# Six places for the first modulation units, the projection weights in four transfers, and the bias lines inside its first tile

## The chip, the cores and the metric

The kernel runs on one core of a Trainium2 chip. The metric is device time in microseconds (us) of one execution. An execution of this kernel is a chain over five engines: TensorE (PE, with its weight loads as PEld), VectorE (DVE), ScalarE (ACT), GpSimd (POOL) and SyncE (SP), which here only issues transfers. Transfers issued by SP and ACT are listed as hardware queues q1 and q10, those issued by POOL as q0; all of them run on the same 16 DMA engines.

## The reference

One decoder layer for 512 prompt tokens and 8 sample tokens, width 1024, all in float32. In short:

```
mod = silu(c) @ w_ada + b_ada            # 9 rows of c, w_ada 1024 x 6144; six parts: sh, sc, g and sh_f, sc_f, g_f
h   = rms_norm(x) * (1 + sc) + sh        # 520 tokens
q, k, v, u = split(h @ w_in)             # w_in 1024 x 1280
attn = sliding window attention with sinks and a relative bias; pool = causal means of u
x   = x + g * (concat(attn, pool) @ w_out)
y   = x + g_f * moe(rms_norm(x) * (1 + sc_f) + sh_f)     # top 4 of 32 experts, w1 1024 x 2048, w2 1024 x 1024
```

The change touches what leads up to `h @ w_in` and that product's first tile of tokens.

## The kernel before, in words

The program has two parts with a barrier of all engines between them: `head`, all up to the routing, and `experts`. Nothing in `experts` is changed. Each engine has its own list of instructions, written out by hand, and runs it in order; semaphores (`wait_ge`, `then_inc`) tie the lists together.

**Modulation.** `w_ada` is loaded in 24 units of 1 MB, each 512 rows by 512 columns; two units make a chunk of 512 modulation columns. Chunks 0 to 3 (units 0 to 7, `WHOLE`) are shift and scale of the mixer and are needed before any projection. `load_ada` (L551) puts unit n into place n modulo 3 (`ADA_SLOTS`) of the ring `m.raw`, and waits from unit 3 on until the products of unit n - 3 are done (`ada_used`). TensorE multiplies a unit in `ada(n)` (L1342, matmul L1351), four products that stand beside each other in a bank; `mod_row(c)` (L1019) adds the bias row and the four partial rows on VectorE (L1028, L1032); `turn_mod(c)` (L1368, transposes L1372) turns the row on TensorE. When chunk 3 is turned, VectorE copies everything to `modT` (L1070) and forms `g1T`. The bias rows come in `m.bada`, 1024 columns at a time, each reload waiting until the rows before have been used.

**Tokens.** The tokens are loaded as four tiles of 128 and one of 8 (`load_x`), normed on ScalarE (L820 to L827, reciprocal on VectorE L1045), turned on TensorE (`turn_x`, L1364) and copied to `hT` by ScalarE (L833) and VectorE (L1048). TensorE's list takes `ada(t)` and `turn_x(t)` in turns, then `ada(5)`.

**Bias lines.** For each of the 8 heads one product of 33 rows by 383 columns (L1389) gives the head's relative bias as a line; VectorE copies it to `m.line` (L1064), with two banks in turn; a ninth product (L1391) gives `bias64`. TensorE's list has these nine between `turn_mod(1)` and `turn_mod(2)`, ahead of `ada(6)` and `ada(7)`. POOL later writes the lines to memory (`skew`, L688) and reads them back shifted (L695) for the scores.

**Projection.** `w_in` comes as one transfer of 5 MB (L580), issued behind unit 7. TensorE waits for it, then runs tile t = 0 to 3: eight steps k, each a product of 512 columns (L1437) and one of 256 (L1438) for q, k and v. VectorE has made `hT` for step k just before (L1082: scale and shift, eight instructions). Then come the samples, and u for all tokens (L1449).

**POOL.** Twelve small tables are loaded at the start (L666). When `w_in` has landed POOL loads the expert biases `m.bb`, clears `yd` in memory, copies caches, and writes `skew`.

## Time and profile before

| | us |
|---|---|
| median of 3 runs | 1385.18 (1381.89, 1385.18, 1388.03) |
| the profiled execution | 1384.42 |
| its span in the profile | 1382.7 |
| PE busy | 1221.5 (88%) |
| DVE busy | 669.8 (48%) |
| ACT busy | 490.1 (35%) |
| POOL busy | 215.4 (16%) |
| DMA, mean | 348 GB/s, 481.25 MB |

The span is what the profile sees of the execution; 1.7 us lie around it. Busy times are sums over the whole span, and stages with quite different limits are mixed in them, so the argument reads stages and waits rather than these sums. "idle before" in a line of the timeline is the time that the engine stood still ahead of it, with what released it; `<-issue` means that nothing in the profile shows what it waited for.

### The profile page before, as it was taken

Reading aid. Unit: us, or ns where it says so; the run is one execution under the profiler, and the core shown is the slowest. Engines: PE = TensorE matmul, PEld = TensorE weight load, DVE = VectorE, ACT = ScalarE, POOL = GpSimd, SP = SyncE. Lnnn points to the kernel's source line nnn. Section 1 sums busy time; section 2 is a strip of 40 time slices with the busy share of each in tenths; the row PEclk is TensorE's granted clock in tenths of the full one; section 3 lists DMA queues with packets and bytes.
Section 4 is the critical chain, followed back from the end, with each engine's and each line's share of the span. In section 5 each row is a group of like instructions: output and inputs, shape, how many; then the busy total and the mean of one; then the engine's idle time right before and its main releaser. Section 6 shows DMA issues by size and latency. Waiting matters only on the chain.

```text
span 1382.7 us, 17472 instructions
## 1 busy us (share of the span) xinstructions
PE 1221.5 (88%) x6463; PEld 725.0 (52%) x6463; DVE 669.8 (48%) x970; ACT 490.1 (35%) x703; POOL 215.4 (16%) x285
## 2 busy tenths in 40 slices
PE   4899779979999979999899889999789999999770
PEld 2364445543565735756674247555457654747320
DVE  2532664453675864543784134435334444837303
ACT  5011342230554633332663033333323343736300
POOL 3211321032111112102211101021111021111001
PEclk9699899989999999999999999999889999999885
DMA  9940686459999999999999999999999999999994
GB/s 297 380 135 5 237 286 228 159 220 400 360 401 366 404 403 389 402 389 344 410 412 401 400 389 406 387 347 405 405 389 400 386 363 411 406 411 403 412 391 181
DMA packets 113658, 481.25 MB, mean 348 GB/s; under 512 B 12497, under 2 KB 13824, under 8 KB 83820
## 3 DMA queue, kind: packets, MB, share of 16 engines
q1 hardware_dynamic: 100460, 451.52, 82.4%
q0 software_dynamic: 12768, 27.47, 7.5%
q10 hardware_dynamic: 344, 1.12, 0.3%
q8 instruction: 53, 0.87, 0.3%
q14 instruction: 33, 0.27, 0.1%
HBM read 463.46 MB, written 24.14 MB: 353 GB/s over the span
## 4 chain that ended last, share of the span: by engine, by line
PE 53%; DMA 13%; SPq 5%; DVE 5%; issue 1%; ACT 1%; POOLq 0%; ACTq 0%; DVEq 0%
PE bank L2302 50%; DMA raw<-in_w 9%; SPq L526 3%; DVE rawr L2141 2%; PE bank L2349 1%; DMA yd<-ost,slot_tok 1%; SPq L536 1%; DMA yd<-gu,slot_tok 1%; PE bank L2326 1%; ACT hi L1970 1%; DVE gu L2105 1%; SPq L532 1%; DMA xg_even<-h2d,slot_tok 0%; DVE gu L2103 0%; DVE yf L2295 0%
## 5 line engine op out<-in xcount | busy, mean ns | idle before, releaser
L2141 DVE TENSOR_TENSOR rawr<-raw,hi 128x1024 fp32r<-128x1024 f32 x288 | 341.5, 1222 | 125.0 <-ACT hi L1970 121.8
L1970 ACT CAST hi<-raw 128x1024 fp32r<-128x1024 f32 x288 | 295.4, 1049 | 153.9 <-PE bank L2302 113.8
L2302 PE MATMUL bank<-raw,xT_even 128*64 128x512 f32 (+1 forms) x704 | 138.0, 613 | 4.8 <-DMA raw<-in_w 4.7
L2302 PE MATMUL bank<-raw,aT 128*32 128x256 f32 (+1 forms) x992 | 109.6, 456 | 14.8 <-DMA raw<-in_w 14.6
L1862 POOL DMA_INDIRECT yd<-ost,slot_tok x31 | 54.4, 1756 | 362.6 <-ACT ost L1953 362.6
L2302 PE MATMUL bank<-raw,xT_odd 128*32 128x512 f32 (+1 forms) x544 | 88.0, 668 | 18.0 <-DMA raw<-in_w 18.0
L2302 PE MATMUL bank<-hi,aTh 128*128 128x512 f32 x240 | 78.7, 410 | 18.8 <-DVE rawr L2141 18.8
L2302 PE MATMUL bank<-hi,xTh_even 128*128 128x512 f32 x256 | 83.3, 407 | 5.3 <-DVE rawr L2141 5.3
L2103 DVE TENSOR_SCALAR gu<-bank 128x512 f32<-128x512 f32 (+1 forms) x50 | 31.4, 628 | 104.8 <-PE bank L2302 104.8
L1938 ACT ACTIVATE gu<-gu 128x512 f32<-128x512 f32 (+1 forms) x50 | 29.2, 583 | 144.1 <-DVE gu L2103 144.1
L2302 PE MATMUL bank<-rawr,xTh_even 128*128 128x512 f32 x256 | 80.1, 394 | 0.0
L2302 PE MATMUL bank<-hi,xTl_even 128*128 128x512 f32 x256 | 79.9, 393 | 0.0
L2302 PEld LDWEIGHTS bank<-raw,aT 128*32 128x32 f32 (+1 forms) x992 | 40.9, 120 | 74.1 <-issue 36.3
L2302 PE MATMUL bank<-hi,xTh_odd 128*128 128x512 f32 x224 | 73.5, 410 | 5.5 <-DVE rawr L2141 5.5
L2302 PE MATMUL bank<-rawr,aTh 128*128 128x512 f32 x240 | 76.3, 400 | 0.0
L2302 PE MATMUL bank<-hi,aTl 128*128 128x512 f32 x240 | 76.1, 399 | 0.0
L2302 PEld LDWEIGHTS bank<-raw,xT_even 128*64 128x64 f32 (+1 forms) x704 | 35.2, 127 | 68.2 <-issue 57.4
L2302 PE MATMUL bank<-rawr,xTh_odd 128*128 128x512 f32 x224 | 70.6, 397 | 0.0
L2302 PE MATMUL bank<-hi,xTl_odd 128*128 128x512 f32 x224 | 69.9, 394 | 0.0
L1953 ACT ACTIVATE ost<-bank,slot_gate 128x512 f32<-128x512 f32 (+1 forms) x43 | 26.0, 633 | 122.6 <-PE bank L2302 111.9
L2159 DVE SCALAR_TENSOR_TENSOR aTl<-bank,aTh 128x512 fp32r<-128x512 f32 x30 | 20.7, 689 | 97.8 <-ACT aTh L1931 97.8
L2302 PEld LDWEIGHTS bank<-hi,aTh 128*128 128x128 f32 x240 | 45.2, 194 | 34.4 <-DVE rawr L2141 23.2
(363 smaller groups left out, 1681.3 us busy)
## 6 DMA issues: line engine op xcount, KB each, us to landing
raw<-in_w SPq DMA_DIRECT2D x356, 1024.0 KB, 18.3
raw<-in_w_ada SPq DMA_DIRECT2D x24, 1024.0 KB, 7.1
raw<-in_w SPq DMA_DIRECT2D x48, 512.0 KB, 11.8
w_in_sb<-in_w_in SPq DMA_DIRECT2D x1, 5120.0 KB, 17.3
w_out_sb<-in_w_out SPq DMA_DIRECT2D x4, 1024.0 KB, 7.1
early<-in_w SPq DMA_DIRECT2D x4, 1024.0 KB, 12.4
xs<-in_x_prompt SPq DMA_DIRECT2D x4, 512.0 KB, 15.8
yd<-zero POOLq DMA_DIRECT2D x4, 512.0 KB, 10.5
```

The source lines that it names most:

```text
L526: sp.dma_start(raw.rearrange("p (k n) -> p k n", k=2), src).then_inc(landed, 16)
L532: sp.dma_start(raw[:, kk * D:(kk + 1) * D].rearrange("p (h c) -> p h c", h=2), src[:, :, j * 512:(j + 1) * 512]).then_inc(landed, 16)
L536: sp.dma_start(raw, src).then_inc(landed, 16)
L1862: gp.indirect_dma_start(yd_of[n], bass.IndirectOffsetOnAxis(ap=m.slot_tok[:, p % 6, b:b + 1], axis=0), out_rows(p, b), None, bounds_check= ...
L1938: nc.scalar.activation(gate, gate, ACT.Silu, scale=ALPHA).then_inc(silu_ready, 1)
L1953: done = nc.scalar.activation(out_rows(p, b)[:, n * w:(n + 1) * w], src, ACT.Copy, scale=m.slot_gate[:, p % 6, b:b + 1])
L1970: nc.scalar.copy(m.hi[:, (2 * n + h) % HI, :], m.raw[:, slot, h * D:(h + 1) * D]).then_inc(hi_done, 1)
L2103: v.tensor_scalar(gate, g, LIMIT, None, ALU.min).then_inc(gmin_ready, 1)
L2105: v.tensor_scalar(up, u, LIMIT, -LIMIT, ALU.min, ALU.max).then_inc(gu_free, 1)
L2141: v.tensor_tensor(m.rawr[slot][:, half], m.raw[:, slot, half], m.hi[:, (2 * n + h) % HI, :].bitcast(F32), ALU.subtract).then_inc(lo_done, 1)
L2159: v.scalar_tensor_tensor(m.aTl[:, k:k + n, :].rearrange("p k n -> p (k n)"), bank[7][:, 0:n * P], 1.0 / ALPHA, m.aTh[:, k:k + n, :].bitcas ...
L2302: return nc.tensor.matmul(out, lhsT, rhs, start=start, stop=stop, skip_group_check=True)
```

## The change

- `w_ada` units 0 to 5 get six places: the three of before and three more in memory that is free at that time (`m.ada_more`). Unit 6 and 7 go to places 0 and 1; units from 8 on rotate over three places as before, and wait for the same products as before.
- SP's list: units 0 to 4 and token tiles 0 to 4 in turns, units 5 to 7, then `w_in` as four transfers of two steps each with a semaphore each, then unit 8. The waits on `c_tr` and on the bias rows between units are gone from this stretch.
- The bias rows for chunks 0 to 3 (2048 columns) are one early transfer on ACT's queue into `m.bada_01`; `m.bada` serves the later chunks.
- TensorE's list: `ada(6)`, `turn_mod(2)`, `ada(7)`, `turn_mod(3)` directly behind `turn_mod(1)`. The eight bias lines are taken into projection tile 0, two ahead of steps 0, 2, 4 and 6, behind a wait for `modT`; `bias64` stands between tile 0 and tile 1. Banks 6 and 7 hold the lines.
- VectorE's list: `mod_row(3)` right behind `mod_row(2)`; the line copies go between the `hT` scalings, two behind every second one; the samples' scaling comes behind the eight.
- POOL: five of the twelve tables (`sinks_bc`, `br_bc`, `rec`, `w_pool`, `sp`) are loaded behind `m.bb`. `m.bb` and ScalarE's cast of it also wait for chunk 3's row, since `m.bada_01` and a unit's place lie in the same memory.
- Some semaphores are merged (`step`, `pool_step`, `kn_raw`).

```diff
-ADA_SLOTS = 3
+ADA_SLOTS, ADA_MORE = 3, 3
+        m.ada_more = [at(f"ada_more{n}", [P, 2048], F32, H0 + place) for n, place in enumerate((81216, 89600, 41216))]
+        m.bada_01 = at("bada_01", [9, 2 * D], F32, H0 + 68928)
+    def ada_place(n):
+        late = ADA_SLOTS + ADA_MORE
+        return n if n < late else (n - late) % ADA_SLOTS
@@ load_ada
-                if n >= ADA_SLOTS:
-                    sp.wait_ge(s.ada_used, n - ADA_SLOTS + 1)
+                earlier = [k for k in range(n) if ada_place(k) == ada_place(n)]
+                if earlier:
+                    sp.wait_ge(s.ada_used, earlier[-1] + 1)
@@ SP
-            for n in range(ADA_SLOTS):
-                load_ada(n)
-                load_x(n)
-            for t in range(ADA_SLOTS, TT):
-                load_x(t)
-            sp.wait_ge(s.c_tr, 1)
-            load_bada(0)
-            for n in range(ADA_SLOTS, ADA):
+            for t in range(TT):
+                load_ada(t)
+                load_x(t)
+            load_ada(TT)
+            for n in range(TT + 1, WHOLE):
                 load_ada(n)
-                if n == 7:
-                    sp.dma_start(m.w_in[:], i["w_in"][0].rearrange("(k p) n -> p k n", p=P)).then_inc(s.win_in, 16)
+            for n in range(4):
+                sp.dma_start(m.w_in[:, 2 * n:2 * n + 2, :],
+                             i["w_in"][0, 2 * n * P:(2 * n + 2) * P, :].rearrange("(k p) n -> p k n", p=P)
+                             ).then_inc(win_in[n], 16)
+            for n in range(WHOLE, ADA):
+                load_ada(n)
@@ POOL
-            gp.wait_ge(s.win_in, 16)
+            for n in range(4):
+                gp.wait_ge(win_in[n], 16)
+            gp.wait_ge(s.mr_ready, WHOLE // 2)
             gp.dma_start(m.bb[:, 0:2 * D], i["b1"][0]).then_inc(s.bb_in, 16)
             gp.dma_start(m.bb[:, 2 * D:3 * D], i["b2"][0]).then_inc(s.bb_in, 16)
+            for dst, src in (sinks_bc, br_bc, rec, w_pool, sp):      # the five pairs, shortened here
+                gp.dma_start(dst, src).then_inc(s.small_in, 16)
@@ ACT
+            act.dma_start(m.bada_01[:], i["b_ada"][0:1, 0:2 * D].to_broadcast([9, 2 * D])).then_inc(s.bada_in, 16)
+            act.wait_ge(s.ada_used, WHOLE)
+            act.wait_ge(s.mr_ready, WHOLE // 2)
             act.wait_ge(s.bb_in, 32)
@@ DVE
-            v.wait_ge(s.small_in, 12 * 16)
+            v.wait_ge(s.small_in, 7 * 16)
 ...
             mod_row(2)
-            for h in range(NH):
-                v.wait_ge(s.line_tr, h + 1)
-                if not h:
-                    v.wait_ge(s.c_tr, 1)
-                v.tensor_copy(m.line[:, h, :], bank[4 + h % 2][:, 0:LINE]).then_inc(s.line_ready, 1)
-            v.wait_ge(s.bias64_tr, 1)
-            v.tensor_copy(m.bias64[:], bank[6][0:64, 0:P + 1]).then_inc(s.bias64_ready, 1)
             mod_row(3)
 ...
             for k in range(KC):
                 v.tensor_scalar(m.hT[:, k, 0:SEQ], m.hT[:, k, 0:SEQ], m.g1T[:, k, 8:9], m.modT[:, k, 8:9],
                                 ALU.mult, ALU.add).then_inc(s.h_ready, 1)
+                if k % 2:
+                    for h in (k - 1, k):
+                        v.wait_ge(s.line_tr, h + 1)
+                        v.tensor_copy(m.line[:, h, :], bank[6 + h % 2][:, 0:LINE]).then_inc(s.line_ready, 1)
@@ PE
-            pe.wait_ge(s.rel_ready, 1)
-            for h in range(NH):                    # the eight lines, then bias64
-            turn_mod(2)
-            ada(6)
-            ada(7)
-            turn_mod(3)
+            ada(6)
+            turn_mod(2)
+            ada(7)
+            turn_mod(3)
+            def bias_line(h):
+                if h >= 2:
+                    pe.wait_ge(s.line_ready, h - 1)
+                mm(bank[6 + h % 2][:, 0:LINE], m.relrep[:, h, :], m.oh_line[:, 0:LINE], start=True,
+                   stop=True).then_inc(s.line_tr, 1)
-            pe.wait_ge(s.win_in, 16)
-            pe.wait_ge(s.bias64_ready, 1)
+            pe.wait_ge(s.rel_ready, 1)
+            pe.wait_ge(s.modT_ready, 1)
             for t in range(TT):
 ...
                 if t == 1:
-                    pe.wait_ge(s.modT_ready, 1)
+                    pe.wait_ge(s.line_ready, NH)
+                    mm(bank[6][0:64, 0:P + 1], ...rel64..., m.oh_s[:], start=True, stop=True).then_inc(s.bias64_tr, 1)
+                    pe.wait_ge(s.bias64_ready, 1)
 ...
                 for k in range(KC):
                     if not t:
+                        if not k % 2:
+                            bias_line(k)
+                            bias_line(k + 1)
+                        pe.wait_ge(win_in[k // 2], 16)
                         pe.wait_ge(s.h_ready, k + 1)
```

## Rows read from the trace of the kernel before

**Rows 1.** Page part 2, busy tenths in 40 slices of 34.6 us

```profile
PE   4899779979999979999899889999789999999770
...
DMA  9940686459999999999999999999999999999994
```

**Rows 2.** Chain that ended last, its first piece: start us, us, what

```profile
305.80 0.04 issue
```

**Rows 3.** Windows: busy us of PE, PEld, DVE, ACT, POOL, clock, DMA share, GB/s

```profile
100.00:120.00 20.00, 20.00 (x112) 9.53 (x111) 6.80 (x18) 5.23 (x15) 3.64 (x7) 1.00 0.03 9
```

**Rows 4.** Waits of SyncE's queue, 0 to 300 us: total, times, longest

```profile
SPq L556 <- PE bank L1351: 160.0, 16, 89.3
...
SPq L536 <- PE bank L1577: 18.8, 1, 18.8
```

**Rows 5.** Timeline, 35 to 60 us: start, us, engine, line, tiles, idle before

```profile
35.15 0.51 SPq L580 DMA_DIRECT2D w_in_sb<-in_w_in  x1
...
39.56 8.03 PE L1389 MATMUL bank<-oh_line_sb,relrep 33*128 33x383 f32 x12 [1.80 <-DVE line L1064]
...
46.34 0.56 DVE L1064 COPY line<-bank 128x383 f32<-128x383 f32 x1 [0.72 <-PE bank L1389]
...
48.65 3.24 PE L1351 MATMUL bank<-raw,cT 128*9 128x512 f32 x16
...
52.68 2.12 DVE L1032 TENSOR_TENSOR mrow<-mrow,bank 9x512 f32<-9x512 f32 x3
52.75 0.52 POOL L678 DMA_DIRECT2D bb<-in_b  x1 [40.71 <-DMA w_in_sb<-in_w_in]
...
55.48 0.31 DVE L1070 COPY modT<-bank 128x144 f32<-128x144 f32 x1 [0.69 <-PE bank L1372]
...
56.23 4.22 DVE L1082 TENSOR_SCALAR hT<-hT,g1T,modT 128x512 f32<-128x512 f32 x8
...
56.92 2.04 PE L1437 MATMUL bank<-w_in_sb,hT 128*128 128x512 f32 x2 [1.47 <-DVE hT L1082]
```

**Rows 6.** Timeline: bb_lo, fourth step of tile 0, the tile's first reader

```profile
62.75 3.35 DVE L1089 TENSOR_TENSOR bb_lo<-bb,bb_hi 32x3072 fp32r<-32x3072 f32 x1 [2.16 <-ACT bb_hi L843]
...
63.20 1.02 PE L1437 MATMUL bank<-w_in_sb,hT 128*128 128x512 f32 x2
...
69.85 0.60 ACT L870 ACTIVATE sq<-bank 128x512 f32<-128x512 f32 x1 [7.14 <-PE bank L1438]
```

**Rows 7.** Timeline: third and fourth token tile on ScalarE, relrep on VectorE

```profile
22.27 1.06 ACT L820 ACTIVATE xn<-xs 128x1024 f32<-128x1024 f32 x1 [1.81 <-DMA xs<-in_x_prompt]
...
25.50 1.06 ACT L820 ACTIVATE xn<-xs 128x1024 f32<-128x1024 f32 x1
...
34.10 0.68 DVE L1058 COPY relrep<-relb 33x1024 f32<-33x1024 f32 x1
```

**Rows 8.** Busy time in steps of 2 us, columns as in Rows 3

```profile
28.00:30.00 2.00, 0.87 (x11) 0.81 (x8) 0.14 (x1) 2.00 (x4) 0.00 (x0) 1.00 1.04 385
...
44.00:46.00 2.00, 2.00 (x4) 0.90 (x3) 0.90 (x2) 0.00 (x0) 0.00 (x0) 0.50 1.01 412
...
60.00:62.00 2.00, 2.00 (x5) 0.95 (x4) 0.59 (x2) 2.00 (x1) 1.11 (x2) 0.59 1.03 409
```

**Rows 9.** DMA queues, 5 to 20 us: packets, MB, share of 16 engines

```profile
q0 software_dynamic: 480, 0.70, 31.4%
```

**Rows 10.** Timeline of SyncE, the issue of unit 6

```profile
28.15 0.37 SPq L556 DMA_DIRECT2D raw<-in_w_ada  x1
```

**Rows 11.** Tile raw, the landing of unit 6, us after its issue

```profile
DMA to landing us min/median/max: 6.9/6.9/6.9
```

**Rows 12.** Timeline: the bias lines read back, and the first scores

```profile
79.28 4.27 POOL L695 DMA_DIRECT2D bias<-skew  x8 [18.17 <-DMA skew<-line]
...
138.96 1.41 DVE L1157 SCALAR_TENSOR_TENSOR Pb<-bank,bias 128x256 f32<-128x256 f32 x4
```

**Rows 13.** Timeline of SyncE, the issue of the sample tile

```profile
6.83 2.11 SPq L549 DMA_DIRECT2D xs<-in_x_sample  x1
```

More of the change, by code:

```diff
@@ L379, in head @@
     s.recip_ready = signal("recip_ready")
-    s.gate_step = signal("gate_step")
     s.warm = signal("warm")
@@ L387, in head @@
     s.bb_in = signal("bb_in")
-    s.win_in = signal("win_in")
+    win_in = [signal(f"win_in{n}") for n in range(4)]
     s.wout_in = signal("wout_in")
@@ L407, in head @@
     s.ada_used = signal("ada_used")
-    s.g1_ready = signal("g1_ready")
-    s.hT_half = signal("hT_half")
     s.h_ready = signal("h_ready")
@@ L426, in head @@
     s.hrs_ready = signal("hrs_ready")
-    s.qn_raw = signal("qn_raw")
     s.kn_raw = signal("kn_raw")
@@ L440, in head @@
     s.spT_ready = signal("spT_ready")
-    s.spool_step = signal("spool_step")
     s.dTs_ready = signal("dTs_ready")
@@ L465, in head @@
     s.s_tr = signal("s_tr")
-    s.s_soft = signal("s_soft")
     s.s_step = signal("s_step")
@@ L502, in head @@
     x_in = [signal(f"x_in{t}") for t in range(TT)]
-    ada_in = [signal(f"ada_in{n}") for n in range(ADA_SLOTS)]
+    ada_in = [signal(f"ada_in{n}") for n in range(ADA_SLOTS + ADA_MORE)]
     h2_free = [signal(f"h2_free{n}") for n in range(2)]
@@ L511, in head, with ada_unit, ada_landed @@
     WHOLE = 8
+    def ada_place(n):
+        late = ADA_SLOTS + ADA_MORE
+        return n if n < late else (n - late) % ADA_SLOTS
+    def ada_unit(n):
+        a = ada_place(n)
+        return m.raw[:, a, :] if a < ADA_SLOTS else m.ada_more[a - ADA_SLOTS][:]
+    def ada_landed(n):
+        return 16 * (1 + sum(ada_place(k) == ada_place(n) for k in range(n)))
     ada_bank = [bank[2 + c % 2] if c < 4 else bank[2] for c in range(CHUNKS)]
@@ L1021, in mod_row @@
                 v.wait_ge(s.ada_used, 2 * c + 2)
-                v.wait_ge(s.bada_in, 16 * (c // 2 + 1))
+                v.wait_ge(s.bada_in, 16 * max(c // 2, 1))
+                shift = m.bada_01[:, c * 512:c * 512 + 512] if c < 4 else m.bada[:, c % 2 * 512:c % 2 * 512 + 512]
                 if c >= 2:
@@ L1083, in _ @@
                                 ALU.mult, ALU.add).then_inc(s.h_ready, 1)
-            v.wait_ge(s.hT_half, 1)
+                if k % 2:
+                    for h in (k - 1, k):
+                        v.wait_ge(s.line_tr, h + 1)
+                        v.tensor_copy(m.line[:, h, :], bank[6 + h % 2][:, 0:LINE]).then_inc(s.line_ready, 1)
+            step(v.tensor_tensor(m.hT[:, :, SEQ:TOK], m.hT[:, :, SEQ:TOK], m.g1T[:, :, 0:NS], ALU.mult))
             v.tensor_tensor(m.hT[:, :, SEQ:TOK], m.hT[:, :, SEQ:TOK], m.modT[:, 0:8, 0:NS],
                             ALU.add).then_inc(s.h_ready, 1)
+            v.wait_ge(s.bias64_tr, 1)
+            v.tensor_copy(m.bias64[:], bank[6][0:64, 0:P + 1]).then_inc(s.bias64_ready, 1)
             v.wait_ge(s.bb_hi_done, 1)
@@ L1219, in sample_softmax @@
                 v.wait_ge(s.bias64_ready, 1)
[L1220 to L1224 removed]
+                step(v.scalar_tensor_tensor(m.P64[:], bank[3][0:64, 0:P], HD ** -0.5, m.bias64[:, 0:P], ALU.mult,
+                                            ALU.add))
+                step(v.tensor_reduce(m.s64[:, 0:1], m.P64[:], AX_X, ALU.max))
                 v.tensor_tensor(m.s64[:, 0:1], m.s64[:, 0:1], m.bias64[:, P:P + 1], ALU.max).then_inc(s.s_step, 1)
@@ L1351, in ada @@
                     last = mm(ada_bank[c][32 * k:32 * k + 9, :], m.cT[:, 4 * half + k, :],
-                              m.raw[:, n % ADA_SLOTS, k * 512:(k + 1) * 512], start=half == 0, stop=half == 1)
+                              ada_unit(n)[:, k * 512:(k + 1) * 512], start=half == 0, stop=half == 1)
                 last.then_inc(s.ada_used, 1)
@@ L1418, in _ @@
                 if t == 1:
-                    pe.wait_ge(s.modT_ready, 1)
+                    pe.wait_ge(s.line_ready, NH)
+                    mm(bank[6][0:64, 0:P + 1], m.rel64[:].rearrange("p b h -> p (b h)"), m.oh_s[:], start=True,
+                       stop=True).then_inc(s.bias64_tr, 1)
+                    pe.wait_ge(s.bias64_ready, 1)
                 if t == TP:
```

64 lines of the change are left out of this document (24 added, 40 removed).

## The prediction

> **What bounds the kernel now.** I read the 40 slices first. DMA is at 9 tenths nearly everywhere from the twelfth slice on, where the experts run; ahead of that it sinks to 0, while PE stays at 7 to 9 [rows 1]. So the two parts have different limits. The chain that ended last starts at 305.80 us [rows 2]: it says nothing of the head, because a barrier lies there, and the head needs a reading of its own. Between 100 and 120 us PE is busy for 20.00 of 20 us at a clock of 1.00 while DMA moves 9 GB/s [rows 3]: whatever reaches this stage earlier leaves it earlier by as much. From there on the transfers of the head, those of the experts' first weights too, wait for PE (160.0 us on the modulation products, 18.8 us on the output products [rows 4]), so they are tied to the head's work and not to a time of day. I therefore count a shift of the projection's end in full as a shift of the whole, and look at the 70 us before it.
>
> There the timeline shows this order. `w_in` is issued only at 35.15, behind unit 7, since each unit waits for a place and a bias row. PE meanwhile runs bias lines until 47.6, then takes units 6 and 7 until 51.9. VectorE's row 3 ends at 54.80, PE turns it, VectorE copies `modT` from 55.48 to 55.79, and the first projection product starts at 56.92. `w_in` had landed by 52.7, which is when POOL is released [rows 5]. So two things end almost together, 52.7 for the weights and 55.79 for `modT`; the change has to move both. The fourth step of tile 0 starts at 63.20 and ACT reads the tile at 69.85 [rows 6]: five steps in 6.45 us with a signal of 0.2, 1.25 to 1.29 us each (a step's two products follow each other so), and tile 1 starts at about 69.65.
>
> **When modT is ready.** Its chain in the changed lists: token tile 3 on ACT, tile 4, rows 0 and 1, `relrep`, row 2, `turn_mod(2)`, `ada(7)`, row 3, `turn_mod(3)`, copy. Tile 2 landed at 22.27, and ACT, not the transfer, held tile 3 until 25.50; behind row 1 `relrep` ran from 34.10 to 34.78 [rows 7]. In the new order tile 3 comes behind one more unit, 2.7 us (1.05 MB at the 385 GB/s of 28 to 30 us [rows 8]). Against that, five tables leave this stretch. POOL's queue took 31.4% of 15 us, 4.7 us of all engines' time [rows 9]; these five have four fifths of its bytes but fewer than half its transfers, and I take 2.7 us, with 0 and 4.7 as bounds. The two cancel but for the order: tile 2 lands at 19.6, unit 3 at 22.3, tile 3 some 1.4 us (0.52 MB) to 2.0 us later, say 24.0. ACT starts it 1.5 us earlier than before, and this shift goes through to `relrep`, which ends at 33.3.
>
> A row is four additions; three take 2.12, so four take 2.83: row 2 ends at 36.1. Turning takes 0.7 (from 54.80 to 55.48): 36.8. `ada(7)` takes 3.24 / 2 = 1.6: 38.4. Row 3: 41.3; turned 42.0; copied 42.4 (0.31 and a signal) [rows 5]. The last two units must be there: unit 6 was issued at 28.15 and landed 6.9 us later, at 35.05 [rows 10, 11], in a queue that never ran dry; unit 7 now follows without a gap, so 35.05 + 2.7 - 2.7 = 35.05, against 36.8 needed. `modT` at 42.4 is 13.4 us earlier. With no relief from the tables it is 45.1, with the full 4.7 us about 40.9.
>
> **When the weights are ready.** 5.24 MB at the 412 GB/s of 44 to 46 us, when only `w_in` and a unit behind it were moving [rows 8], is 12.7 us, in four parts of 3.2: 38.2, 41.4, 44.6, 47.8. Step 0 starts at about 45, step 6 at about 58. All four are hidden, the last by 10 us; if that cover were gone, each us late would be a us lost. The busy share of DMA is 1.04 from 28 to 30 us, while one unit follows the other [rows 8]: I see no gap between transfers. The Trainium skill, DMA: Bandwidth & Descriptors, section "Anatomy of one DMA", gives each transfer a fixed cost of about 2.0 us beside its bytes. Were it paid four times in series, the last part would be there at some 56 us by that estimate, still early.
>
> **What tile 0 now costs.** At the high clock a step is 1.29 us, so eight are 10.3. Six lines took 8.03 us at the low clock [rows 5], 1.34 each; a line has 383 columns where a step has 768, so by the step's price it is 0.64 at the high clock, 5.1 for eight. That price is not in the trace; its bounds are 5.1 and, at the price seen, 10.7. Cold time comes on top. In tile 0 of before the first three steps took 6.28 us (56.92 to 63.20) in place of 3.87: 2.4 us lost, the clock at 0.59 on average from 60 to 62 [rows 8]. Now two lines go ahead at low clock (2.6 us, 1.3 lost), and the rise comes as long after step 0 as before or a little sooner: 3.2 lost in sum, bounds 0 (the clock is already up) and the first rival below. Between the tiles stands `bias64`: two short passes, a copy of 0.3 us and two signals, 0.8 us on the path (0.4 to 1.3). VectorE has 2.2 us of work in a pair of steps (two of the eight scalings that took 4.22, two copies of 0.56 [rows 5]), PE 3.84, so no step waits for it.
>
> Tile 1 starts at 42.4 + 5.1 + 10.3 + 3.2 + 0.8 = 61.8 instead of 69.65: 7.8 us earlier. In short: 13.4 us gained by the order, 5.6 given back in tile 0, for tile 0 with its start took 13.9 before and takes 19.4 now.
>
> **Edits that I cost at nothing.** The expert biases `bb` are issued at 47.8 instead of 52.75. Before, ACT was through with their cast at 62.7 (its read at 69.85 has 7.14 us of idle time before it), and VectorE's `bb_lo` took 3.35 us [rows 6]; both are now queued ahead of tile 0's norms. By the same distance the cast ends at 57.8, under tile 0. The norms' result is turned only after tile 1, at 72, so the cast may end as late as 64 before it costs anything. The lines are complete at 60 instead of 47; their return from memory was waited for until 79.28, the first scores come at 138.96 [rows 12], about 131 then: some 40 us of cover. The five tables land around 55 and are read behind 110. The merged semaphores change waits of under 0.1 us.
>
> **The rivals.**
> - *The lines hold the clock down (slower).* From 44 to 46 PE was busy for 2.00 of 2 us, with lines only, at 0.50 of the clock, 1.2 GHz [rows 8]: that work did not raise it. Mixed with the steps it may keep tile 0 slow all the way: 15.4 us of work become 30.8 and tile 1 starts at 42.4 + 30.8 + 1.2 = 74.4, 4.8 us later than before: 1390. It decides from about 22 us of low clock on. Against it, steps outweigh lines two to one, and the clock was up again by the fourth step of before. The Trainium skill, TensorE: Matmul & The Clock Gate, section "What's actually happening", says that the clock follows how busy PE has been, and would let the lines alone raise it; this trace disagrees, with PE busy throughout at 0.50. By that rule this rival could not occur. Chance 8 in 100.
> - *The units don't run ahead, or the gain is lost behind (no change).* SP needed 2.11 us to issue the small sample tile [rows 13], so its queue may take only some transfers at a time; and a wait that I read as hidden may surface in the attention stage. If `modT` moves by only 6 to 8 us, 5.6 are given back: 1383 to 1385. Against it, unit 6 landed from a queue that was full anyway. Chance 20.
> - *The clock is up when the lines begin.* `ada(7)` and the turns come close ahead of them. Then the 3.2 us go too: 1374.2. Chance 10.
> - The forecast, with the bounds of tables and `bias64`: 5 to 9.5 us gained, 1375.7 to 1380.2. Chance 60; 2 for the rest.
>
> **How the numbers follow.** The profiled execution took 1384.42, 0.76 below the median 1385.18. 1384.42 - 7.8 + 0.76 = 1377.4. The three runs of before spread by 6 us, so a median can be off by 1 or 2. The range, 1372.5 to 1385, takes in the early clock and most of the second rival, and leaves out the first. A change of 0.5% is 6.9 us, about what a measurement of this kernel tells from none, and the forecast lies just beyond it: of its 60, 38 are faster by more than that; with 9 of the early clock and 1 more this is 0.48. Slower by as much is only the first rival's neighbourhood, and what I don't see: 0.09. The rest is 0.43.
>
> **What would show it.** In the trace after: `w_in`'s last part landed by 48; units 6 and 7 not waited for by PE; `modT` near 42.4; the clock rising within 7 us of the first line; ACT's first read of the projection near 61.2, the same distance from tile 1's start to the barrier as before (236 us), and the chain from the barrier on unchanged. A `modT` later than 46, a tile 0 longer than 22 us, or a distance grown by over 2 us makes the prediction wrong, and names the step.

## The result, and the profile after

| | median, us | runs | ratio to before, 95% interval |
|---|---|---|---|
| before | 1387.72 | 12 (1381.89 to 1392.48) | |
| after | 1378.62 | 12 (1373.40 to 1387.07) | 0.9942 [0.9921, 0.9963] |

The change saves 8.1 us by the ratio (5.1 to 11.0), 9.1 us between the medians. The prediction was 1377.4, in a range of 1372.5 to 1385. The profiled execution of after took 1374.44 us with a span of 1372.7 (before: 1384.42 and 1382.7), so those two profiles lie 10 us apart. As the marks below show, 3.6 us of that arise far behind the stretch that was edited.

Page part 2 of after, busy tenths in 40 slices of 34.3 us, answers to [rows 1]:

```profile
PE   5899779969999979997999889998789999999871
...
DMA  9930866479999999999999999999999999999995
```

At this width nearly nothing has moved. The same stretches limit the kernel, and what changed lies inside the first two slices. The timeline of after shows it (start us, us, engine, line, tiles, count, idle time before and its releaser), and answers to [rows 5, 7, 10]:

```profile
17.44 5.34 SPq L566 DMA_DIRECT2D raw<-in_w_ada  x2
...
19.74 1.06 ACT L835 ACTIVATE xn<-xs 128x1024 f32<-128x1024 f32 x1 [0.66 <-DMA xs<-in_x_prompt]
...
22.83 7.13 SPq L587 DMA_DIRECT2D w_in_sb<-in_w_in  x4
...
23.73 1.06 ACT L835 ACTIVATE xn<-xs 128x1024 f32<-128x1024 f32 x1 [0.66 <-DMA xs<-in_x_prompt]
...
36.52 1.04 PE L1357 MATMUL bank<-raw,cT 128*9 128x512 f32 x8
38.34 2.12 DVE L1049 TENSOR_TENSOR mrow<-mrow,bank 9x512 f32<-9x512 f32 x3
40.52 0.59 PE L1378 MATMUL bank<-ident,mrow 9*128 9x9 f32 x4 [2.96 <-DVE mrow L1049]
41.15 0.31 DVE L1080 COPY modT<-bank 128x144 f32<-128x144 f32 x1 [0.69 <-PE bank L1378]
41.60 2.89 PE L1400 MATMUL bank<-oh_line_sb,relrep 33*128 33x383 f32 x4 [0.49 <-DVE modT L1080]
44.42 2.07 PE L1449 MATMUL bank<-w_in_sb,hT 128*128 128x512 f32 x2
...
48.15 0.52 POOL L685 DMA_DIRECT2D bb<-in_b  x1 [38.96 <-DMA w_in_sb<-in_w_in]
```

Token tiles 2 and 3 now start at 19.74 and 23.73 instead of 22.27 and 25.50. Units 6 and 7 carry no wait for a transfer. `modT` is copied by 41.46 instead of 55.79, and the last quarter of `w_in` releases POOL at 48.15 instead of 52.75. Then comes the price, in tile 0. The same view a little further on, which answers to [rows 6]:

```profile
49.45 1.55 PE L1400 MATMUL bank<-oh_line_sb,relrep 33*128 33x383 f32 x4
50.93 1.12 PE L1449 MATMUL bank<-w_in_sb,hT 128*128 128x512 f32 x2
...
53.71 1.55 PE L1400 MATMUL bank<-oh_line_sb,relrep 33*128 33x383 f32 x4
...
57.97 1.55 PE L1400 MATMUL bank<-oh_line_sb,relrep 33*128 33x383 f32 x4
...
62.23 0.43 PE L1425 MATMUL bank<-oh_s_sb,rel 33*64 33x129 f32 x2
62.33 0.60 ACT L887 ACTIVATE sq<-bank 128x512 f32<-128x512 f32 x1 [3.87 <-PE bank L1450]
62.91 3.34 DVE L1101 TENSOR_TENSOR bb_lo<-bb,bb_hi 32x3072 fp32r<-32x3072 f32 x1
63.03 1.13 PE L1449 MATMUL bank<-w_in_sb,hT 128*128 128x512 f32 x2 [0.38 <-DVE bias L1098]
```

Pairs of lines start 4.26 us apart at the high clock: two lines and two steps. Busy time of after in steps of 2 us (PE, PEld, DVE, ACT, POOL, granted clock, DMA share, GB/s), beside [rows 8]:

```profile
38.00:40.00 2.00, 0.00 (x0) 0.00 (x0) 1.90 (x4) 0.00 (x0) 0.00 (x0) 0.69 1.01 410
...
46.00:48.00 2.00, 2.00 (x5) 1.01 (x4) 0.00 (x0) 0.00 (x0) 0.00 (x0) 0.50 1.05 391
48.00:50.00 2.00, 2.00 (x6) 1.02 (x5) 0.00 (x0) 0.00 (x0) 1.85 (x4) 0.75 1.05 382
50.00:52.00 2.00, 2.00 (x7) 0.84 (x6) 1.52 (x4) 0.00 (x0) 2.00 (x4) 1.00 1.04 385
```

The clock had fallen while PE waited for VectorE's row 3 (1.00 from 36 to 38, 0.69 on average from 38 to 40), and rose at 49, 7.4 us after the first line began. So `modT` to tile 1 takes 21.57 us (41.46 to 63.03). Tile 1 started at 69.65 before, so it starts 6.6 us earlier, not 14. The start of tile 1 before, and the first turn of the norms' result before and then after:

```profile
69.65 1.02 PE L1437 MATMUL bank<-w_in_sb,hT 128*128 128x512 f32 x2
```

```profile
79.97 0.60 PE L1408 MATMUL bank<-ident,qn 128*128 128x128 f32 x4
```

```profile
73.46 0.60 PE L1413 MATMUL bank<-ident,qn 128*128 128x128 f32 x4
```

Behind tile 1 the projection is the same: PE's first score product comes at 130.25 and before at 136.76, 6.5 us apart. But the chain behind the barrier starts at 295.68 (before 305.80 [rows 2]), 10.1 us apart:

```profile
295.68 0.04 issue
```

From there to the end both take 1077 us. The other 3.6 us arise between the scores and the barrier. Windows from 130 to 205 us, before and then after:

```profile
130.00:205.00 75.00, 57.56 (x340) 33.68 (x339) 45.99 (x79) 28.26 (x92) 22.25 (x22) 0.86 0.66 229
```

```profile
130.00:205.00 75.00, 55.01 (x375) 33.26 (x373) 47.80 (x83) 30.77 (x96) 22.28 (x22) 0.93 0.68 241
```

The clock averages 0.86 in one and 0.93 in the other: some 21 and 10.5 us at the lower level (75 x 0.14 / 0.5 and 75 x 0.07 / 0.5). The change edits nothing here but a few merged waits, and those gave no gain that can be told (the last experiment). From PE's first score product to the output product the profiles of this case take 77.3 to 84.8 us, and the time goes with the clock: 77.3 and 77.5 us at a mean of 0.93, 84.5 and 84.8 us at 0.82. The order does not follow the edits in any plain way. The two shortest are after and the lines in one block; the two longest are the two kernels whose scores come first, and whether that is more than chance isn't shown.

### The profile page after: what moved, and what is told of

It is laid out like the page before. It is cut to its first block, busy times and chain, and to the rows that moved or that the text cites. A ratio compares the mean times of both kernels' runs of the same rounds, so it can differ in the third digit from the quotient of the medians.

```text
span 1372.7 us, 17486 instructions
## 1 busy us (share of the span) xinstructions
PE 1222.7 (89%) x6463; PEld 724.1 (53%) x6463; DVE 668.9 (49%) x970; ACT 490.3 (36%) x703; POOL 212.9 (16%) x285
## 4 chain that ended last, share of the span: by engine, by line
PE 55%; DMA 11%; SPq 5%; DVE 5%; issue 1%; ACT 1%; POOLq 0%; ACTq 0%
PE bank L2315 53%; DMA raw<-in_w 8%; SPq L535 3%; DVE rawr L2154 2%; DMA yd<-ost,slot_tok 1%; PE bank L2362 1%; SPq L545 1%; PE bank L2339 1%; DMA yd<-gu,slot_tok 1%; SPq L541 1%; ACT hi L1983 1%; DVE gu L2118 1%; DVE gu L2116 0%; DMA yf<-yd 0%; DVE yf L2305 0%
## 5 line engine op out<-in xcount | busy, mean ns | idle before, releaser
L2315 PE MATMUL bank<-raw,aT 128*32 128x256 f32 (+1 forms) x992 | 114.2, 480 | 10.8 <-DMA raw<-in_w 10.6
L2315 PE MATMUL bank<-raw,xT_odd 128*32 128x512 f32 (+1 forms) x544 | 86.9, 665 | 14.3 <-DMA raw<-in_w 14.2
L2315 PE MATMUL bank<-hi,xTh_even 128*128 128x512 f32 x256 | 84.8, 414 | 3.8 <-DVE rawr L2154 3.8
```

The source lines that it names most:

```text
L2315: return nc.tensor.matmul(out, lhsT, rhs, start=start, stop=stop, skip_group_check=True)
```

## The experiments

Each kernel was timed 6 to 12 times. The ratios are to the kernel before. Where a kernel is told to be some us slower or faster than after, the medians are meant. The intervals reach 2.4 to 4.8 us to each side. Each of the differences of 2.9 to 4.5 us from after, taken singly, is therefore not clear of noise; the marks in the timeline carry the argument, and the times only agree with it.

**The tables early again.**

```diff
-                             (m.kn_bc[:], i["k_norm"].to_broadcast([P, HD]))):
+                             (m.kn_bc[:], i["k_norm"].to_broadcast([P, HD])),
+                             (m.sinks_bc[:], i["sinks"].to_broadcast([P, NH])),
...
+                             (m.sp[:], i["state_pool"][0].rearrange("b t c -> (b t) c"))):
```

> The changed kernel with all twelve small tables loaded at the start again. Theory (my sum): the five tables take 2.7 us of all engines' time ahead of token tiles 1 to 3, for which ScalarE waits in the changed kernel (its squares start at 15.75, 19.74 and 23.73 us, each behind a transfer), so modT moves from 41.46 to about 44 and the whole loses 2 to 2.7 us against the changed kernel: some 1380.5 where that one takes 1378.6. Rival: the tables only filled gaps of the transfers, and modT moves by under 0.7 us.

1381.49, ratio 0.9962 [0.9945, 0.9979]: 2.9 us slower than after. `modT` ends at 45.90, 4.4 us later, more than the 2.7 I had taken and near my upper bound of 4.7. DMA queue 0 (packets, MB, share of 16 engines) from 5 to 20 us, with the tables early and in after:

```profile
q0 software_dynamic: 480, 0.70, 25.1%
```

```profile
q0 software_dynamic: 224, 0.14, 9.4%
```

The windows from 10 to 14 us, in the same order:

```profile
10.00:14.00 4.00, 0.47 (x4) 0.00 (x0) 0.16 (x1) 3.26 (x5) 1.95 (x8) 1.00 1.01 270
```

```profile
10.00:14.00 4.00, 0.03 (x4) 0.00 (x0) 0.16 (x1) 3.33 (x5) 0.00 (x0) 1.00 0.95 351
```

With 0.56 MB more of tables the engines move 270 in place of 351 GB/s, and 285 in place of 396 in the next 4 us, while busy for as much of the time or more: 8 us in which some 0.8 MB less move. The Trainium skill, DMA: Bandwidth & Descriptors, section "Queues, rings and completion order", says that an engine takes turns between its queues packet by packet; that fits SyncE's transfers sharing each engine with POOL's. It gives no price; the runs do, 4 us on the third token tile (23.77 against 19.74), and as much on the weights:

```profile
52.14 0.52 POOL L691 DMA_DIRECT2D bb<-in_b  x1 [40.08 <-DMA w_in_sb<-in_w_in]
```

The last quarter of `w_in` comes 4.0 us later than in after, hardly earlier than the 52.75 of before. No step waits for it here, since its step comes later still. The norms' result is first turned at 77.56, 4.1 us later than in after.

**The lines ahead of the modulation turns again.**

```diff
+            for h in range(NH):
+                bias_line(h)
...
+            turn_mod(2)
             ada(6)
-            turn_mod(2)
             ada(7)
             turn_mod(3)
...
-                        if not k % 2:
-                            bias_line(k)
-                            bias_line(k + 1)
```

> The changed kernel with the eight bias lines and bias64 back between turn_mod(1) and turn_mod(2), units 6 and 7 behind them; everything else as changed. Theory: the lines stand on TensorE's path ahead of modT there: modT at about 52.5, tile 0 short again (13.9 us with its start), tile 1 starts at 66.5 instead of 63.03: 3.5 us slower than the changed kernel, so that a good half of the gain was the lines' place. Rival: inside tile 0 the lines cost as much as ahead of it, because they stretch the low clock: within 1 us of the changed kernel, or faster than it.

1381.60, 0.9964 [0.9946, 0.9981], 3.0 slower than after; `modT` at 52.34 and the norms' result turned 2.4 us later:

```profile
75.85 0.60 PE L1417 MATMUL bank<-ident,qn 128*128 128x128 f32 x4
```

I had expected 3.5 us. With weights and tables early but the lines where they were, some two thirds of the gain remain (4.1 of 6.5 us at this mark): the order of the lines is worth 2.4 us there and 3.0 by the medians, not the 10.9 by which it moves `modT`.

**`w_in` in one transfer.**

```diff
-            for n in range(4):
-                sp.dma_start(m.w_in[:, 2 * n:2 * n + 2, :],
...
+            sp.dma_start(m.w_in[:], i["w_in"][0].rearrange("(k p) n -> p k n", p=P)).then_inc(win_in[0], 16)
```

> The changed kernel with w_in as one transfer and one semaphore. Theory: it lands at about 47.9 us as the last of the four does now, the first step waits for it instead of starting at 44.42: 3.5 us slower than the changed kernel (0.5 less where the pause is used by line work, up to 1 more where the clock rises later). Rival: four transfers cost more in the queue than they give, or the rise of the clock at a fixed instant gives the loss back, and the difference is under 1 us.

1381.91, 0.9966 [0.9949, 0.9983], 3.3 slower. The first step of tile 0 waits for the whole of the weights:

```profile
48.17 2.07 PE L1445 MATMUL bank<-w_in_sb,hT 128*128 128x512 f32 x2 [2.94 <-DMA w_in_sb<-in_w_in]
```

It starts 3.75 us later than in after, while the whole landed no sooner in one piece than in four (48.1 and 48.15). The norms' result is turned 3.6 us later.

**Three places in place of six.**

```diff
-ADA_SLOTS, ADA_MORE = 3, 3
+ADA_SLOTS, ADA_MORE = 3, 0
```

> The changed kernel with ADA_MORE = 0: units rotate over three places, the order of the transfers and the early bias rows are kept. Theory: units wait for products, as unit 7 for those of unit 4 (done at 29.8 us), so it lands at 37 or 38 where 36.5 is needed: modT later by 0.5 to 1.5 us, the last quarter of w_in by 2 to 3 us at about 51, still ahead of its step at 59: 0.5 to 1.5 us slower than the changed kernel. Rival: the six places are the heart of the change, and without them most of the 8 us go.

1378.21, 0.9942 [0.9921, 0.9963], the ratio of after to four digits; `modT` at 40.02, if anything earlier. I missed here: the three further places bring nothing that these runs can tell. Units 3 to 5 are issued as places come free, at 9.94, 17.74 and 22.23, `w_in` only at 28.89, and yet no product waits for it, and its last quarter is there as early as in after:

```profile
48.12 0.52 POOL L685 DMA_DIRECT2D bb<-in_b  x1 [38.92 <-DMA w_in_sb<-in_w_in]
```

So the places are not what brings the weights. The trace of before shows what held them: the waits of SyncE's queue from 0 to 60 us (total, times, longest), and the window from 34 to 36 us:

```profile
SPq L560 <- DVE mrow L1032: 7.9, 2, 5.5
```

```profile
34.00:36.00 2.00, 1.60 (x10) 1.15 (x7) 0.78 (x2) 0.00 (x0) 0.00 (x0) 0.58 0.34 52
```

SyncE stood for 5.5 us ahead of the second set of bias rows (issued at 33.99), until VectorE had used the first; unit 7 and `w_in` are behind it in the list, and DMA fell to 52 GB/s. With three places and the early bias rows it moves 415 GB/s in the same window, in after 412. The early bias rows remove this wait; no run takes them back by themselves.

**The lines between tiles 0 and 1.** The same eight lines, in one block behind the eight steps.

```diff
                 if t == 1:
+                    for h in range(NH):
+                        bias_line(h)
                     pe.wait_ge(s.line_ready, NH)
...
-                        if not k % 2:
-                            bias_line(k)
-                            bias_line(k + 1)
```

> The changed kernel with the eight lines as one block between tile 0 and tile 1, where the clock is up, and step 0 right behind modT. Theory (a pair of lines inside tile 0 costs 1.68 us at the high clock, 0.84 a line and not the 0.64 of my sum, because the array changes between operands of 33 and of 128 rows; in a block the two banks bound them instead, at some 0.75): tile 1 starts about 1 us earlier than in the changed kernel, since no line runs at the low clock: 1 us faster, within what can be told. Rival (lines keep the clock down when they stand among the steps): the rise comes earlier by a window without them, 2 to 3 us faster.

1382.05, 0.9965 [0.9946, 0.9983]: 3.4 us slower than after, where I had expected a gain. Timeline of PE, and windows:

```profile
54.93 1.02 PE L1447 MATMUL bank<-w_in_sb,hT 128*128 128x512 f32 x2
55.79 0.59 PE L1448 MATMUL bank<-w_in_sb,hT 128*128 128x256 f32 x2
56.32 8.59 PE L1399 MATMUL bank<-oh_line_sb,relrep 33*128 33x383 f32 x16
65.56 0.69 PE L1426 MATMUL bank<-oh_s_sb,rel 33*64 33x129 f32 x2 [0.65 <-DVE line L1092]
66.62 2.07 PE L1447 MATMUL bank<-w_in_sb,hT 128*128 128x512 f32 x2 [0.38 <-DVE bias L1097]
```

```profile
56.00:58.00 2.00, 1.99 (x7) 0.80 (x6) 0.65 (x2) 2.00 (x1) 0.44 (x1) 1.00 1.05 313
58.00:60.00 2.00, 2.00 (x5) 0.96 (x6) 1.38 (x3) 1.16 (x4) 0.00 (x0) 0.78 1.02 396
60.00:62.00 2.00, 2.00 (x4) 0.93 (x3) 0.75 (x2) 0.00 (x0) 0.00 (x0) 0.50 0.96 389
```

The steps alone run from 42.82 to 56.3, as expected. Then comes the block of lines, products of 33 rows each, and the clock falls from 1.00 to 0.50 with PE busy throughout; tile 1 begins at the low level (2.72 us a step in place of 1.29). This is the mechanism of my first rival, met in another place: in a block of lines the clock fell, with steps between the lines (in after, from 50 to 62 us) it stayed up.

**Lines 0 and 1 in PE's pause of 2.96 us ahead of `turn_mod(3)`** (banks 0 and 1, free by then).

```diff
             ada(7)
+            bias_line(0)
+            bias_line(1)
             turn_mod(3)
...
-                        if not k % 2:
+                        if k and not k % 2:
                             bias_line(k)
```

> The changed kernel with lines 0 and 1 moved ahead of turn_mod(3), where TensorE stands still for 2.96 us behind unit 7, into banks 0 and 1. Theory: they fit (2.56 us at the low clock, less at the high), modT does not move, and step 0 starts at 42.3 instead of 44.42 after the start: 2.1 us faster than the changed kernel. Rival: the steps meet the low clock for as much longer and give half of it back: 1 us; or turn_mod(3) is held up: no gain.

1374.11, 0.9901 [0.9871, 0.9932]. By the medians that is 4.5 us under after, where I had expected 2.1; the six runs lie in two groups, 1369.3 to 1370.1 and 1378.1 to 1379.6, so this median is a weak one. The trace:

```profile
37.33 2.92 PE L1396 MATMUL bank<-oh_line_sb,relrep 33*128 33x383 f32 x4
```

The pair takes 2.92 us at 37.33, `turn_mod(3)` is not delayed (40.35), step 0 follows `modT` at 42.28, and the norms' result is turned 2.7 us earlier than in after.

**PE kept busy in that pause with eight unused products.**

```diff
+            for _ in range(8):
+                mm(bank[5][:, 0:P], m.ident[:], m.ident[:], start=True, stop=True)
             turn_mod(3)
```

> The changed kernel with eight more products of the identity by itself (128 columns, nobody reads them) in the same gap ahead of turn_mod(3): work that changes nothing but TensorE's activity. Theory (the low clock costs 3.6 us in tile 0, 7.85 us for two lines and two steps in place of 4.26): the lines and steps run at the high clock for part of it, 1 to 3.6 us faster than the changed kernel, with step 0 at 43.2 where the clock is up. Rival: the pause for turn_mod(3) and the lines themselves let the clock fall again before the steps: same as the changed kernel, or 1 us slower where the eight take 3.4 us and delay turn_mod(3).

1378.98, 0.9942 [0.9921, 0.9964]. Nothing is gained, where I had expected 1 to 3.6 us: steps 0 and 1 are at the low level all the same, and `modT` to tile 1 takes 21.3 us. The products did hold the clock up for longer:

```profile
40.00:42.00 2.00, 1.27 (x6) 0.93 (x7) 1.42 (x5) 0.00 (x0) 0.00 (x0) 0.85 1.01 412
```

It is at 1.00 until about 41.4, where in after it fell at 38.8. But then it falls 0.3 us into the first lines, ahead of the first step.

**Lines of one column.** Only the first column of each line is computed and is spread over the tile, so the bias table holds other values and the expert part does other work (1526.13 in all); only the first 60 us are read.

```diff
-                mm(bank[6 + h % 2][:, 0:LINE], m.relrep[:, h, :], m.oh_line[:, 0:LINE], start=True,
+                mm(bank[6 + h % 2][:, 0:1], m.relrep[:, h, :], m.oh_line[:, 0:1], start=True,
```

> The changed kernel with each of the eight lines cut to its first column (the bias table is then wrong beyond it; the copies, waits and transfers stay). It prices the lines in tile 0. Theory: eight lines cost 6.7 us at the high clock and 1.1 more at the low one; without their columns tile 0 is 6.5 to 7.5 us shorter, so that tile 1 starts at about 56; the steps then wait for VectorE, which has 2.2 us of work a pair against 2.58. Rival (the lines also hold the clock down): 9 us or more, with the rise within 4 us of step 0.

```profile
46.43 0.60 PE L1400 MATMUL bank<-oh_line_sb,relrep 33*128 33x1 f32 x4
46.96 1.13 PE L1449 MATMUL bank<-w_in_sb,hT 128*128 128x512 f32 x2
...
49.74 0.60 PE L1400 MATMUL bank<-oh_line_sb,relrep 33*128 33x1 f32 x4
```

`modT` to tile 1 takes 16.74 us, 4.83 less, where I had expected 6.5 to 7.5. For pairs are still 3.31 us apart, where two bare steps take 2.58: 0.73 us a pair is left with practically no columns. Of the 1.68 us of a pair in after, 0.95 are columns and 0.73 go to the four short passes themselves and to coming back, which this run doesn't separate (a step's first two products 1.12 in place of 1.02).

**The lines' move alone, on the kernel before.**

```diff
-            pe.wait_ge(s.rel_ready, 1)
-            for h in range(NH):
...
                 if h >= 2:
                     pe.wait_ge(s.line_ready, h - 1)
-                mm(bank[4 + h % 2][:, 0:LINE], m.relrep[:, h, :], m.oh_line[:, 0:LINE], start=True,
+                mm(bank[6 + h % 2][:, 0:LINE], m.relrep[:, h, :], m.oh_line[:, 0:LINE], start=True,
                    stop=True).then_inc(s.line_tr, 1)
...
+                        if not k % 2:
+                            bias_line(k)
+                            bias_line(k + 1)
+                        pe.wait_ge(s.win_in, 16)
```

> The kernel before with one part of the change alone: the two bias lines ahead of every second step of tile 0 (and ada(6), turn_mod(2), ada(7), turn_mod(3) before the tile, bias64 between tiles 0 and 1). One w_in transfer behind unit 7, three places, bias rows and tables as before. Theory: modT comes some 9 to 11 us earlier (45 to 47 us), since the eight lines and most of the wait behind them leave its chain, but w_in still lands at about 52, so the first step waits for it, and tile 0 is longer by the lines; tile 1 starts at 69 to 71 us, and the time is that of the kernel before within 1.5 us (1386 to 1389). Rival: w_in was not late, or PE gets through tile 0 faster than I count, and moving the lines is worth 3 us or more by itself (1384 or less).

1389.18, 1.0014 [0.9991, 1.0036]: no gain. `modT` at 46.05, and then:

```profile
52.95 2.08 PE L1442 MATMUL bank<-w_in_sb,hT 128*128 128x512 f32 x2 [3.86 <-DMA w_in_sb<-in_w_in]
```

Tile 1 starts at 72.26, 2.6 us later than before and a little outside the 69 to 71 that I had expected. So the move pays nothing by itself, since the first step then waits for the weights. The reverse does not hold: the early transfers without the move, in the run with the lines ahead, keep some two thirds of the gain.

**Three places, lines 0 and 1 in the pause.** The one-line edit of the three places, on top of the kernel with two lines in the pause.

> e6_lines_in_gap (lines 0 and 1 in PE's pause ahead of turn_mod(3)) with three places for the units in place of six, as in e4_three_places. Theory: the six places bring nothing, so modT comes at about 40 us and tile 1 starts at about 59 us, 1.4 us earlier than in e6_lines_in_gap; the time is equal to e6_lines_in_gap or 1 us shorter, 1373 to 1374.5, some 4.5 us less than the changed kernel. Rival: with three places something behind the head (the later modulation units, bb) is late, as the equal times of e4_three_places and the changed kernel may say: then it stays 1 us or more above e6_lines_in_gap.

1378.11, 0.9926 [0.9897, 0.9955]. I missed: `modT` came at 42.11, not 40, and tile 1 at 62.45. By itself 42.11 speaks against three places, 40.02 above for them; two profiles of six places gave 41.46 and 41.29. The three places fall to both sides of that, 2 us apart, so these profiles show no difference. The time is 4.0 above the same kernel with six places, with intervals that overlap; whether any of it is real stays open.

**Only two lines left in tile 0.** `relrep` behind VectorE's first reciprocal, lines 0 to 3 among the token tiles (banks 4 to 7), lines 4 and 5 in the pause, three places. The edit is shown against after.

```diff
+                if t in (1, TP - 1):
...
+                    bias_line(t - 1)
+                    bias_line(t)
...
-                        if not k % 2:
-                            bias_line(k)
-                            bias_line(k + 1)
+                        if k == 2:
+                            bias_line(6)
+                            bias_line(7)
```

> Three places; relrep is made right behind VectorE's first reciprocal; lines 0 to 3 are computed behind unit 1 and unit 3, among the token tiles, lines 4 and 5 in PE's pause ahead of turn_mod(3), and only lines 6 and 7 inside tile 0, ahead of its third step. Theory: a pair of lines in tile 0 costs 1.7 us, relrep on modT's chain 0.7; against e10_gap_three two more pairs leave tile 0 (3.4 us) and relrep leaves the chain (0.7 us): tile 1 starts at 55 to 56 us, the time is about 3.5 to 4 us under e10_gap_three, 1369.5 to 1371. Rival: part of it is given back, because the low clock falls on steps in place of lines (up to 2 us more in tile 0), or because the lines delay the token tiles: then tile 1 starts at 57 to 58 us and the time is 1.5 to 2 us under e10_gap_three.

1374.85 (1373.31 to 1376.97), 0.9903 [0.9868, 0.9937]. `modT` at 40.58; tile 1:

```profile
56.23 1.13 PE L1471 MATMUL bank<-w_in_sb,hT 128*128 128x512 f32 x2 [0.38 <-DVE bias L1108]
```

That is 6.8 us earlier than in after and near the theory's mark, but the time is 3.3 under the kernel above, not the 1369.5 to 1371 that I had expected, and no better than the one with two lines in the pause and six places. Both beat before. Against after their medians are 3.8 and 4.5 us lower with intervals that overlap, and between the two these runs can't choose.

**The merged waits alone, on the kernel before.**

```diff
-                ins.then_inc(s.gate_step, 1)
+                ins.then_inc(s.pool_step, 1)
...
-                v.scalar_tensor_tensor(m.P64[:], bank[3][0:64, 0:P], HD ** -0.5, m.bias64[:, 0:P], ALU.mult,
-                                       ALU.add).then_inc(s.s_soft, 1)
-                v.wait_ge(s.s_soft, 1)
+                step(v.scalar_tensor_tensor(m.P64[:], bank[3][0:64, 0:P], HD ** -0.5, m.bias64[:, 0:P], ALU.mult,
+                                            ALU.add))
```

> The kernel before with the merged waits of the change alone: the five counters gate_step, g1_ready, hT_half, spool_step and s_soft are gone and their instructions go through the shared step counters, qn_raw's wait is replaced by kn_raw's, and the sample part of hT is scaled behind the eight prompt parts. Order, places and transfers as before. The timed gain of the change is 9.1 us between the two medians, its tile 1 starts only 6.5 us earlier. Theory: these merges are worth nothing and the 2.6 us are scatter of the attention stage, so the time is that of the kernel before within 1 us (ratio's interval holds 1.000) and tile 1 starts at 69.6 us within 0.5. Rival: the merges shorten VectorE's and GpSimd's chains in the attention stage and are worth 2 to 3 us, 1385 to 1386.

1387.57, 1.0005 [0.9986, 1.0023]: no gain that can be told. But its profile missed the mark: ACT reads tile 0 at 72.72, 2.9 us later than in the other profile of this order. The cause lies ahead of every edited instruction. Token tile 1 (counted from 0) starts here at

```profile
19.55 1.06 ACT L814 ACTIVATE xn<-xs 128x1024 f32<-128x1024 f32 x1 [6.12 <-DMA xs<-in_x_prompt]
```

and at 17.14 before. So with the tables early the landings themselves scatter. Over the four profiles with early tables ACT starts token tile 2 at 21.89, 22.27, 23.77 and 25.09; over the nine of full size with late tables, at 18.91 to 20.43. The profile that the prediction was worked out from was one of the two quicker ones.

**All together.** First turn of the norms' result (10.4 us behind tile 1's start where the clock is up) and median time:

| kernel | `modT` | first turn | median |
|---|---|---|---|
| before | 55.79 | 79.97 | 1387.72 |
| merged waits alone | 59.34 | 82.84 | 1387.57 |
| lines' move alone | 46.05 | 82.69 | 1389.18 |
| lines in a block | 41.83 | 80.08 | 1382.05 |
| tables early | 45.90 | 77.56 | 1381.49 |
| `w_in` in one | 42.19 | 77.05 | 1381.91 |
| lines ahead | 52.34 | 75.85 | 1381.60 |
| after | 41.46 | 73.46 | 1378.62 |
| two lines in the pause, three places | 42.11 | 72.88 | 1378.11 |
| eight unused products | 41.00 | 72.72 | 1378.98 |
| three places | 40.02 | 71.89 | 1378.21 |
| two lines in the pause | 41.29 | 70.79 | 1374.11 |
| two lines left in tile 0 | 40.58 | 66.66 | 1374.85 |

A straight line through these has a slope of 0.9 us of time for each us of the first turn, and single kernels lie up to 3 us off it. `modT` predicts the time badly (46.05 with 1389, 52.34 with 1382), the first turn behind tile 1 well.

At the first turn, where the whole change is worth 6.5 us, taking back the tables costs 4.1, the parts of `w_in` 3.6 and the lines' order 2.4. Together that is more than the whole, so these are not shares to be added: what one part is worth depends on the others being there.

## Why the prediction was right, step by step

- *Where a us of the head goes.* I counted the shift of tile 1 in full, and the table bears it out. The distance from tile 1 to the barrier was to stay at 236 us; it was 232.65. It is no constant of the kernel: over the profiles of this case it is 232.6 to 241.6 us, mostly with how long the clock is down in the attention stage. After's is the shortest of all thirteen, so its profile of 1374.44 is a lucky one.
- *`modT`.* Predicted 42.4, measured 41.46. Token tile 2 came at 19.74 for 19.6, tile 3 at 23.73 for 24.0, row 2 ended at 36.12 for 36.1. The last agreement is in part luck: `relrep` ended at 32.77, 0.5 us sooner than predicted, and VectorE then waited 0.52 us for unit 5's products, which took 1.90 us at the low clock and are not in the predicted chain. The 0.9 us lie behind that: unit 7's products took 1.04 and row 2's turn 0.42, at the high clock, where I had taken 1.6 and 0.7 from rows at the low one.
- *The tables* were mis-sized: 4.4 us of `modT` in the run that puts them back, against 2.7. On token tile 2 the averages of the four profiles with early tables and the nine with late ones are 23.3 and 19.6, 3.7 us apart. It did not show in `modT`, because the profile of before, which I counted from, had an early set of landings: two errors that nearly cancel.
- *The weights.* Parts by 47.8, measured 48.15, and no step waited. One reading behind it was wrong: unit 6 of before did not land from a queue that never ran dry, for nothing had been issued behind it and DMA's share was 0.92 from 32 to 34 us and 0.34 from 34 to 36. It cost the sum nothing, since both units were early. The Trainium skill, DMA: Bandwidth & Descriptors, section "Anatomy of one DMA", gives about 2.0 us of fixed cost for each transfer, fitted on transfers that GpSimd issues (these are SyncE's), and puts most of it down to the confirmation at the end. Paid four times in series it would have made 56, an estimate by that figure. The trace rules the series out: four transfers ended when one did (48.15 and 48.1).
- *Tile 0.* Predicted 19.4 us from `modT` to tile 1, measured 21.57 = 0.14 start + 10.32 eight steps + 6.72 lines + 3.59 low clock + 0.80 `bias64`. The lines are the mis-sized term: 4 pairs of 1.68 in place of 5.1 in all, since I priced them by columns alone and 0.73 us of a pair is not in its columns. The columns themselves came cheaper than priced, 0.95 in place of 1.28 us a pair. The low clock (3.2 predicted) was nearly right and `bias64` (0.8) right. So tile 1 comes at 63.03, not 61.8, and gains 6.6 us instead of 7.8 in these two profiles.
- *The rivals.* The first, that the lines hold the clock down through tile 0, did not occur: the clock rose with the second step. Its mechanism is real, as the block of lines shows. The Trainium skill, TensorE: Matmul & The Clock Gate, section "What's actually happening", lets the clock follow how busy PE has been; the block, where PE was busy 2.00 of 2 us while the clock fell, disagrees, as [rows 8] did for the rise. The second did not occur either: SyncE was held for 5.49 us by one issue; the engines' share was 1.11 from 6 to 10 us and 0.95 from 10 to 14, with a dip to 0.85 from 10 to 12, and no unit behind it was waited for. The third, the clock being up when the lines begin, failed: it fell during the wait for row 3, and eight further products in the pause put the fall off by 2.6 us only, to the first lines.
- *The edits at nothing.* The cast of `bb` ended at 58.47 for 57.8, and `bb_lo` started at 62.91, where it lies under tile 1; VectorE's first reading of the scores came at 132.54 for about 131 (138.96 before [rows 12]); the merged waits showed no gain (1.0005, 0.9986 to 1.0023). I counted the six places as needed for unit 7, and they are not: three do the same.
- *The signs that I had named.* ACT's first read of the projection came at 62.33 for 61.2. The clock rose 7.4 us after the first line, where I had said within 7. `modT` before 46, tile 0 under 22 us (21.57) and a distance to the barrier that did not grow all held.
- *The size.* 7.8 was predicted, 8.1 measured by the ratio, 6.6 on tile 1 in the profiles. That the forecast of 1377.4 came within 1.2 us of 1378.62 owes something to this: before itself measured 1387.72 over 12 runs where the prediction started from 1385.18 over three. The step from 6.6 to 8.1 lies inside the interval. The scatter of the early landings would account for it (the four profiles average 23.3 for token tile 2, 1 us behind the one I used), but this is argued and not shown.

## What to carry to other kernels

Follow a gain to the instruction that the next stage starts with: here 14.3 us on `modT` became 6.6 us on tile 1, because the work moved off the one chain landed on the other, and only the second mattered. Put moved work into a pause that exists (two lines in PE's wait were worth 2.7 us of tile 1, and 4.5 of time by medians whose intervals overlap) before placing it between working steps. Bytes that are read late but fetched early, in many small rows, slowed the transfers that were waited for by 4 us here: look for them first. Look also for an issuing queue that stands at a small transfer with large ones behind it: 5.5 us there let the engines run dry.

## What the runs showed of the hardware

- Products with 33 rows neither raised the clock (8.03 us of them, at 0.50 from 40 to 48 us [rows 5, 8]) nor held it (8.59 us in a block, 1.00 to 0.50), with PE busy throughout; alternated with 128-row steps they did not bring it down (1.00 from 50 to 62 us).
- Going from 128-row steps to a pair of 33-row products and back cost 0.73 us with one column each.
- SyncE's queue took 5.49 us to issue one token tile while several units were outstanding ahead of it (7.71 us for the same transfer with the tables early):

```profile
7.70 5.49 SPq L558 DMA_DIRECT2D xs<-in_x_prompt  x1
13.23 0.60 SPq L566 DMA_DIRECT2D ada_more<-in_w_ada  x1
```

With three places the same transfer took 2.00 us, and `modT` (40.02) and the weights (48.12) came within the scatter of the other profiles: the queue was blocked, the engines hardly (0.95 from 10 to 14 us).
- Of the kernel with two lines in the pause, three runs took 1369.3 to 1370.1 us at a mean granted clock of 0.943 to 0.944, and three 1378.1 to 1379.6 at 0.933 to 0.934. It is no rule for every kernel here: with the lines ahead the fastest run (1376.56) had 0.931 and the slowest (1383.99) 0.941.
